# Griffin/Mamba trunk on one Trainium2 core: the first mixer's projection moved to the 512-column form

## What is computed

```python
def rglru_mixer(u, w_in, conv_w, conv_b, w_gate_r, b_gate_r, w_gate_i, b_gate_i, lam, w_out):
    xy = u @ w_in                                  # 2048 -> 4096: xr and yg
    xr, yg = jnp.split(xy, 2, axis=-1)
    yg = jax.nn.gelu(yg, approximate=True)
    xr = causal_dwconv(xr, conv_w, conv_b)         # 4 taps along the sequence
    xb = xr.reshape(bsz, S, LRU_HEADS, LRU_BLOCK)  # 8 heads of 256
    r = jax.nn.sigmoid(jnp.einsum('bshi,hij->bshj', xb, w_gate_r) + b_gate_r).reshape(bsz, S, LRU_WIDTH)
    i = jax.nn.sigmoid(jnp.einsum('bshi,hij->bshj', xb, w_gate_i) + b_gate_i).reshape(bsz, S, LRU_WIDTH)
    log_a = -LRU_C * r.astype(jnp.float32) * jax.nn.softplus(-lam.astype(jnp.float32))
    a = jnp.exp(log_a)
    mult = jnp.sqrt(-jnp.expm1(2.0 * log_a))
    bterm = mult * (i * xr).astype(jnp.float32)
    _, hs = lax.associative_scan(_lin_combine, (a, bterm), axis=1)
    return (hs.astype(u.dtype) * yg) @ w_out
```

## Time and profile before

| | us |
|---|---|
| median of 3 runs | 2684.93 |
| profiled execution, its own time | 2686.58 |
| its span, first to last instruction | 2684.9 |
| TensorE matmul busy | 2660.2 (99%) |
| VectorE busy | 1993.9 (74%) |
| ScalarE busy | 1394.8 (52%) |
| GpSimd busy | 282.4 (11%) |
| stage A1 | 8 to 227 us of the span |

### The profile page before, as it was taken

The page is one execution under the profiler, slowest core; times in us unless marked ns, Lnnn a source line. Parts: engine busy times, 40 slices in busy tenths (PEclk is TensorE's granted clock), DMA queues, the critical chain, the costliest instruction groups (busy, mean ns, idle before and its releaser), DMA issues.

```text
span 2684.9 us, 47929 instructions
## 1 busy us (share of the span) xinstructions
PE 2660.2 (99%) x16895; PEld 2399.2 (89%) x16895; DVE 1993.9 (74%) x2782; ACT 1394.8 (52%) x1924; POOL 282.4 (11%) x314
## 2 busy tenths in 40 slices
PE   8999999999999999999999999999999999999998
PEld 8999888888888888899998999988888888888887
DVE  7788776665666678888896788978666556667776
ACT  6776444444444445556764567644444444444454
POOL 1001300000000111100001000032000000001211
PEclk9999999999999999999999999999999999999999
DMA  6545555556655566555555555555555665555564
GB/s 217 180 169 191 180 196 189 190 173 188 204 190 190 194 189 198 188 175 189 182 187 187 197 181 184 188 186 189 191 189 173 188 204 191 189 189 175 188 202 138
DMA packets 157054, 502.54 MB, mean 187 GB/s; under 512 B 16848, under 2 KB 25360, under 8 KB 156816
## 3 DMA queue, kind: packets, MB, share of 16 engines
q1 hardware_dynamic: 156864, 501.04, 57.3%
q10 hardware_dynamic: 80, 0.07, 0.0%
HBM read 498.88 MB, written 2.16 MB: 187 GB/s over the span
## 4 chain that ended last, share of the span: by engine, by line
PE 89%; DVE 5%; ACT 3%; issue 1%; DMA 1%; SPq 0%; DVEq 0%; ACTq 0%
PE bank L408 51%; PE bank L410 26%; PE bank L390 4%; PE bank L392 4%; PE bank L391 4%; DVE wlo L904 2%; ACT whi L615 1%; DMA wraw<-in_A 1%; DVE arena L1114 1%; PE bank L576 0%; ACT L691 0%; DVE R L1005 0%; ACT arena L691 0%; ACT arena L700 0%; PE bank L580 0%
## 5 line engine op out<-in xcount | busy, mean ns | idle before, releaser
L408 PE MATMUL bank<-R,whi 128*128 128x512 f32 x5984 | 2084.9, 393 | 0.2 <-DVE wlo L904 0.2
L410 PE MATMUL bank<-R,wlo 128*128 128x256 f32 x5984 | 1674.1, 280 | 0.0
L904 DVE TENSOR_TENSOR wlo<-wraw,whi 128x1024 fp32r<-128x1024 f32 (+2 forms) x1008 | 1164.0, 1161 | 560.2 <-ACT whi L615 558.9
L615 ACT ACTIVATE whi<-wraw 128x1024 fp32r<-128x1024 f32 (+2 forms) x1008 | 984.1, 983 | 891.4 <-PE bank L410 794.1
L408 PEld LDWEIGHTS bank<-R,whi 128*128 128x128 f32 x5984 | 1120.4, 187 | 251.6 <-DVE wlo L904 0.6
L410 PEld LDWEIGHTS bank<-R,wlo 128*128 128x128 f32 x5984 | 1130.0, 189 | 0.1
L390 PE MATMUL bank<-R,whi 128*128 128x256 f32 x1376 | 392.9, 286 | 6.4 <-DVE wlo L904 5.3
L392 PE MATMUL bank<-R,wlo 128*128 128x256 f32 x1376 | 389.6, 283 | 0.0
L391 PE MATMUL bank<-R,whi 128*128 128x256 f32 x1376 | 389.3, 283 | 0.0
L390 PEld LDWEIGHTS bank<-R,whi 128*128 128x128 f32 x1376 | 262.4, 191 | 10.9 <-DVE wlo L904 6.7
L391 PEld LDWEIGHTS bank<-R,whi 128*128 128x128 f32 x1376 | 262.5, 191 | 0.2
(11 more groups left out here) (173 smaller groups left out, 1314.9 us busy)
## 6 DMA issues: line engine op xcount, KB each, us to landing
wraw<-in_F SPq DMA_DIRECT2D x352, 512.0 KB, 3.3
wraw<-in_B SPq DMA_DIRECT2D x224, 512.0 KB, 3.3
wraw<-in_A SPq DMA_DIRECT2D x96, 512.0 KB, 3.6
wraw<-in_F SPq DMA_DIRECT2D x128, 384.0 KB, 3.1
wraw<-in_F SPq DMA_DIRECT2D x128, 320.0 KB, 3.2
wraw<-in_PL SPq DMA_DIRECT2D x64, 512.0 KB, 3.7
arena<-cs_rows SPq DMA_DIRECT2D x8, 1024.0 KB, 6.4
arena<-in_gates SPq DMA_DIRECT2D x8, 512.0 KB, 3.7
```

The source lines that it names most:

```text
L408: nc.tensor.matmul(dst.rearrange("p (s t) -> p s t", s=2), whi[:, q % RING, cols], src[:, :, k, :], start=first, stop=False)
L410: mm = nc.tensor.matmul(dst[:, 0:SEQ], wlo[:, q % RING, cols], src[:, 0, k, :], start=False, stop=last)
L615: nc.scalar.activation(whi[:, slot, 0:w * BLOCK], wraw[:, slot, 0:w * BLOCK], ACT.Copy).then_inc(w_hi, 1)
L904: V.tensor_tensor(wlo[:, slot, 0:w * BLOCK], wraw[:, slot, 0:w * BLOCK], whi[:, slot, 0:w * BLOCK].bitcast(F32), ALU.subtract).then_inc(w_ ...
```

## The change

A1 joins WIDE, so its 512 blocks take one 512-column matmul and one of 256 instead of three of 256; banks 2, 3, 0, 1 are filled in both halves. At s = 1, 3, 5, 7 ScalarE now waits for the group's last piece (w_used) and copies the upper half of the bank into a_low (two buffers, a_half); VectorE waits for a_half, adds the lower half and a_low into xpad or yv, waits for its own result, and multiplies by rinv in place. In VectorE's program the yg groups now stand in front of the taps of the same q. tr and ti get two buffers, by hh, and decays waits for y_done of the head before, since av and sq still have one. lru_y moves from s = 7 to s = 1 of the next head, behind decays and gelu_square; y_low from s = 0 to s = 2. In A2 lru_y of the last heads stands at q = 1 and 5 and y_low at 2 and 6. The gate products keep their form. The core of the diff:

```diff
-LAST_HEAD = {0: (0, 1), 1: (2, 3), 2: (4,), 3: (5,), 4: (6,), 5: (7,)}
+LAST_HEAD = {0: (0, 1), 1: (2, 3), 2: (4,), 3: (5,), 4: (6,)}
-WIDE = ("A2", "F1", "F2", "B2")
+WIDE = ("A1", "A2", "F1", "F2", "B2")
...
+        tr = [tr, scratch(512).rearrange("p (j t) -> p j t", j=2)]
+        ti = [ti, scratch(512).rearrange("p (j t) -> p j t", j=2)]
+        a_low = scratch(512).rearrange("p (n t) -> p n t", n=2)
...
 # ScalarE
-                def decays(head):
+                def decays(head, hh):
                     act.wait_ge(gate_t, head * 4 + 2)
+                    if not isinstance(head, int) or head > 0:
+                        act.wait_ge(y_done, head)
...
-                    elif s == 7:
-                        lru_y(head, hh)
...
+                            if q in (1, 5):
+                                lru_y(LRU_HEADS - 2 + q // 5, q // 5)
...
                             head, hh, s = it * 2 + q // 8, q // 8, q % 8
+                            group = ({4: 0, 5: 1, 6: 2, 7: 3} if first and q < 8 else {1: 0, 3: 1, 5: 2, 7: 3}).get(s)
+                            if group is not None:
+                                act.wait_ge(w_used, HEAD_DONE[group] if first and q < 8 else p + 1)
+                                act.wait_ge(bank_free, it * 8 + ph["group0"] + hh * 4 + group + 3)
+                                nc.scalar.activation(a_low[:, group % 2, :], bank[BANKS4[group]][:, SEQ:2 * SEQ], ACT.Copy
+                                                     ).then_inc(a_half, 1)
...
+                            if s == 1 and not first:
+                                lru_y(head - 2, hh)
...
 # VectorE
-                            if q in (0, 6):
+                            if q in (2, 6):
                                 y_low(LRU_HEADS - 2 + q // 6, q // 6)
...
-                            if s == 0 and not first:
+                            if s == 2 and not first:
                                 y_low(head - 2, hh)
...
                             if group is not None:
-                                dve.wait_ge(w_used, HEAD_DONE[group] if first and q < 8 else p - s + 2 * group + 2)
-                                src = BANKS4[group]
-                            if group in (0, 1):
-                                j = group
-                                tile = head * 2 + j
-                                row = xpad[:, j, 3:3 + SEQ]
-                                V.tensor_tensor(row, bank[src][:, 0:SEQ], rinv[:], ALU.mult).then_inc(bank_free, 1)
+                                if group == 2 and not first:
+                                    dve.wait_ge(y_lo, head * 2 - 2)
+                                row = xpad[:, group, 3:3 + SEQ] if group < 2 else yv[:, hh, group - 2, :]
+                                dve.wait_ge(a_half, head * 4 + group + 1)
+                                own.link(V.tensor_tensor(row, bank[BANKS4[group]][:, 0:SEQ], a_low[:, group % 2, :], ALU.add))
+                                V.tensor_tensor(row, row, rinv[:], ALU.mult).then_inc(bank_free, 1)
...
-                            if group in (2, 3):
-                                if group == 2 and not first:
-                                    dve.wait_ge(y_lo, head * 2 - 2)
-                                row = yv[:, hh, group - 2, :]
-                                V.tensor_tensor(row, bank[src][:, 0:SEQ], rinv[:], ALU.mult).then_inc(bank_free, 1)
```

More of the change, by code:

```diff
@@ L239, in trunk @@
         z_t, exp_done, sc_done = sem("z_t"), sem("exp_done"), sem("sc_done")
-        turned = sem("turned")
+        turned, a_half = sem("turned"), sem("a_half")
         y_mm, y_read, ysq_done, gstat_mm, gvar_done, grinv_done = (sem("y_mm"), sem("y_read"), sem("ysq_done"),
@@ L684, in split_dt_weights, with gates @@
                                          ACT.Copy).then_inc(g_hi, 1)
-                def gates(head):
+                def gates(head, hh):
                     act.wait_ge(g_used, head + 1)
-                    for g, dst in ((0, tr), (1, ti)):
+                    for g, dst in ((0, tr[hh]), (1, ti[hh])):
                         for j in range(2):
@@ L693, in gates @@
                                                  scale=0.5).then_inc(gate_t, 1)
[L695 removed]
+                def decays(head, hh):
                     act.wait_ge(gate_t, head * 4 + 2)
+                    if not isinstance(head, int) or head > 0:
+                        act.wait_ge(y_done, head)
                     kk = [apar[:, at(head * 2 + j), 7:8].rearrange("p a b -> p (a b)") for j in range(2)]
                     for j in range(2):
[L700 removed]
+                        nc.scalar.activation(av[:, j, :], tr[hh][:, j, :], ACT.Exp, bias=kk[j], scale=kk[j]).then_inc(a_done, 1)
                     for j in range(2):
[L702 removed]
+                        nc.scalar.activation(tr[hh][:, j, :], tr[hh][:, j, :], ACT.Tanh, bias=kk[j], scale=kk[j]).then_inc(e_done, 1)
                     act.wait_ge(a_done, head * 2 + 2)
@@ L726, in chain_step @@
                     if s == 0:
-                        gates(head)
+                        gates(head, hh)
                     elif s == 1:
-                        decays(head)
+                        decays(head, hh)
                         gelu_square(head, hh)
@@ L1128, in chain_step @@
                         dve.wait_ge(e_done, head * 2 + 2)
-                        V.scalar_tensor_tensor(out=sq, in0=sq, scalar=1.0, in1=tr, op0=ALU.add, op1=ALU.mult
+                        V.scalar_tensor_tensor(out=sq, in0=sq, scalar=1.0, in1=tr[hh], op0=ALU.add, op1=ALU.mult
                                                ).then_inc(s_done, 1)
                         dve.wait_ge(gate_t, head * 4 + 4)
-                        V.scalar_tensor_tensor(out=ti, in0=ti, scalar=1.0, in1=xc[:, hh], op0=ALU.add, op1=ALU.mult
+                        V.scalar_tensor_tensor(out=ti[hh], in0=ti[hh], scalar=1.0, in1=xc[:, hh], op0=ALU.add, op1=ALU.mult
                                                ).then_inc(gated_done, 1)
@@ L1140, in chain_step @@
                         dve.wait_ge(mult_done, head + 1)
-                        V.tensor_tensor(ti, ti, sq, ALU.mult).then_inc(input_done, 1)
+                        V.tensor_tensor(ti[hh], ti[hh], sq, ALU.mult).then_inc(input_done, 1)
                         dve.wait_ge(input_done, head + 1)
                         for j in range(2):
-                            own.mark(V.tensor_tensor_scan(tr[:, j, :], av[:, j, :], ti[:, j, :], 0.0, ALU.mult, ALU.add))
+                            own.mark(V.tensor_tensor_scan(tr[hh][:, j, :], av[:, j, :], ti[hh][:, j, :], 0.0, ALU.mult, ALU.add))
                         own.need(own.latest())
-                        V.scalar_tensor_tensor(out=yv[:, hh], in0=tr, scalar=0.25, in1=ge, op0=ALU.mult, op1=ALU.mult
+                        V.scalar_tensor_tensor(out=yv[:, hh], in0=tr[hh], scalar=0.25, in1=ge, op0=ALU.mult, op1=ALU.mult
                                                ).then_inc(y_done, 1)
@@ L1369, in group_norm @@
                                                in1=grms[:], op0=ALU.mult, op1=ALU.mult).then_inc(yn_done, 1)
-                steps(dve, ph, body, own, {"A1": 14, "B1": 25, "F1": 6, "PL": 0, "F2": 4}.get(name, 8))
+                steps(dve, ph, body, own, {"A1": 22, "B1": 25, "F1": 6, "PL": 0, "F2": 4}.get(name, 8))
                 own.close()
```

## The result

The changed kernel takes 2694.36 us in the median of six runs (2692.91 to 2698.36), the kernel before 2684.61 beside it. The ratio is 1.0036, with a 95% interval of 1.0025 to 1.0046: slower by 0.36%. The forecast was 2687.2 us with a range from 2679 to 2692. The profiled execution has a span of 2692.8 us and took 2694.53, 7.95 us more than the profiled one of before. The medians are 9.75 apart: that profiled execution of before was itself 2.0 us above its median, and the one of after 0.2.

What follows compares the result with a forecast made beforehand. A cycle of VectorE and ScalarE was taken to bound A1. Last gates at 227.0 against 224.31, 2.7 us later, less A2's 0.4 gap, 2.3 net, counted from the 2684.93 median: 2687.2 us, range 2679 to 2692.

Steps and rivals of the forecast that it cites:

- a cycle of VectorE and ScalarE: In mid-stage A1 these two engines set the pace; the period goes from 26.19 to 27.13 us a head.
- the link through y: ScalarE's 3.15 us idle before copying y's high half in A1 goes; a longer link through TensorE replaces it.
- ScalarE's copy: Copying half a bank in each A1 group was taken at 0.36 us, between 0.3 and 0.6.
- VectorE's two operations: Each A1 group's added operation was priced at 0.58 us in the loop, 0.46 in the last, unrolled iteration.
- SyncE's and GpSimd's queues are not touched: Transfer queues in A1 and A2: claimed unchanged, graw still waiting for g_lo; moving later y halves costs TensorE nothing.
- the three periods of the loop: Three A1 heads at 27.13 us each, bringing the gates now at 172.38 to 174.0.
- the last two: Two A1 heads of the last iteration at 26.5 us each, ending at 227.0 against 224.31.
- the first iteration: Start of A1: a copy and two second operations cost 1.0 us, head 1's gates at 64.1; after 65.5 means wrong.
- The three late pieces: First iteration of A1: piece 8 waited 0.75 us for lo, and pieces 9 and 10 follow as tightly.
- its 0.4 us: TensorE's gap before 241.73 in A2, made by late decays, was to go.
- (b): Rival: TensorE sets the pace in A1, 25.4 us a head, 2676.4 us, or 2680 with half; chance 0.15.
- (c): Rival: ScalarE's path from the s = 1 copy to hi of s = 2 is longer, period 27.9, 2691.1 us; chance 0.22.

Runs made afterwards that it cites:

- late_copy_graw: Changed kernel with graw issued later and ScalarE's step 1 copy behind decays, the GELU square and lru_y: 2684.00 us, ratio 0.9995.
- after_graw_later: Changed kernel with graw issued three pieces later in SyncE's queue, at step 5 instead of 2: 2690.60 us, ratio 1.0021.
- form_only: Kernel before with the 512-column form, copies and additions in A1, but y's halves unmoved and one set of tr and ti: 2695.90 us, ratio 1.0039.
- late_copy: Changed kernel with ScalarE's step 1 copy behind decays, the GELU square and lru_y, graw not moved: 2693.13 us, ratio 1.0030.
- fold_graw: Changed kernel with graw issued later and the halves added by VectorE alone, without ScalarE's copies and waits: 2684.41 us, ratio 0.9997.
- mixed_one_head: Changed kernel with graw later, the step 1 copy behind decays, GELU square and lru_y, and head 0 in three-matmul form: 2681.53 us, ratio 0.9984.

## Why the prediction was wrong

**Right.** That a cycle of VectorE and ScalarE and not TensorE sets a head's time; that the link through y goes; that the new form is a small gain on TensorE. A block takes 0.353 us in the middle of A1 (late_copy_graw: 25.49 less 2.88 us of gates, over 64), so the form is worth 0.007 x 512 = 3.4 us where TensorE paces, where 5.1 had been taken. The estimate from the table of the Trainium skill ("TensorE: Matmul & The Clock Gate", section Back-to-back issue gap) was 1.3 us; the rows lie between the two. The new operations cost no more than was taken. ScalarE's copy is 375 ns in the mean, and the operation behind it starts 0.25 us after it (131.94 and 132.19), where 0.36 had been taken. VectorE's two operations are 416 and 425 ns, and the second starts 0.45 us after the first (150.39 and 150.84), where 0.58 had been taken in the loop (groups by line and form, 95 to 205 us, ScalarE's and then VectorE's):

```profile
L785 ACT ACTIVATE arena<-bank 128x256 f32<-128x256 f32 x16 | 6.0, 375 | 0.0
```

```profile
L1218 DVE TENSOR_TENSOR arena<-arena,rinv 128x256 f32<-128x256 f32 x16 | 6.8, 425 | 0.5
L1217 DVE TENSOR_TENSOR arena<-bank,arena 128x256 f32<-128x256 f32 x16 | 6.7, 416 | 0.0
```

From hi of step 2 (163.20) to the end of L1012 (177.33) the changed kernel takes 14.13 us, against 14.31 forecast.

**The step that failed** is the sentence "SyncE's and GpSimd's queues are not touched, and graw's transfer waits for g_lo as before". The queue wasn't touched, but what had covered it was: ScalarE's idle time of 3.15 us in front of L722, its wait for y. The prediction took that wait away and counted only the waits that ScalarE has for other engines, and not when the piece lands whose transfer stands behind graw. In the trace of before this could be read, as SyncE's own waits (for L1005, 6.4 us at the longest) and in the row at 151.40. The prediction put all of the 26.78 us of that head to the cycle of VectorE and ScalarE, and some 0.6 of it were the queue's. The queue link makes hi of step 2 start 13.3 us after L1012's end at the head of 150, and 14.2 at that of 121.69, where ScalarE waited 3.7 us for the piece; 12.82 was forecast. It costs the three periods of the loop 1.9 us beyond the forecast (83.3 instead of 81.4) and the last two 1.3 (54.3 instead of 53.0). after_graw_later, with the queue cleared, meets the forecast to 0.16 us a head.

**A term that was too small** is the first iteration. The gates of head 1 start at 65.78 instead of 64.1, behind the 65.5 that the prediction had named as the sign of it. The delay is 2.6 us, in place of 1.0, for which one copy and the second operations of two groups had been counted. The two traces show where it grows: VectorE's lo ahead of head 1's first group starts at 48.80 instead of 47.08, ScalarE's tap behind that group at 50.91 instead of 48.74, and its tap behind the next group at 57.43 instead of 54.80. So 1.7 us had come together by the end of head 0's work, and the second operations of head 1's first two groups added 0.45 each. The three late pieces at 36.82, 40.19 and 43.56 were named, and came as said:

```profile
36.82 0.50 PE L411 MATMUL bank<-R,whi 128*128 128x512 f32 x1 [1.18 <-DVE wlo L917]
...
40.19 0.49 PE L411 MATMUL bank<-R,whi 128*128 128x512 f32 x1 [0.29 <-DVE wlo L917]
...
43.56 0.50 PE L411 MATMUL bank<-R,whi 128*128 128x512 f32 x1 [0.32 <-DVE wlo L917]
```

The head that follows takes 28.35 us, the 28.5 of the forecast, and so 1.5 us of it are left at 94.13.

**The sum of the parts** at the last gate products: 1.5 us from the first iteration, 1.9 from the loop and 1.3 from the last iteration, 4.7 us together, are what lies between 227.0 forecast and 231.74. A2 gave back its 0.4 us as forecast. From the first norm's matmul after A2 to the end the changed kernel takes 0.9 us more than before (2362.0 against 2361.1). Nothing of the change lies there, and the profiles of all kernels lie between 2360.8 and 2362.2, so this is read as scatter. The forecast counted from the median of 2684.93. The profiled execution of before was 1.65 us above that and the one of after 0.17 above its own median, which gives the last 1.5 us of the 7.2 by which 2694.36 lies over 2687.2.

**The rivals.** (b) was wrong for the change as it is, and names the period once both links are out. (c) said slower by another mechanism, ScalarE's path dearer than taken; its prices didn't come. The link that came had no rival of its own, and the range had no room for it.

**A stretch at the lower clock.** In the changed kernel the gate products of head 1 take 4.43 us instead of 2.9, most of the 24 matmuls starting 0.21 us after each other instead of 0.12:

```profile
66.54 0.41 PE L395 MATMUL bank<-R 128*128 128x256 f32 x1
66.75 0.41 PE L393 MATMUL bank<-R 128*128 128x256 f32 x1
```

The busy time by engine of that window, with the granted clock behind GpSimd's (x0), gives the cause:

```profile
66.50:69.50 3.00, 3.00 (x16) 3.00 (x15) 1.74 (x4) 2.97 (x4) 0.00 (x0) 0.50 0.93 343
```

The granted clock was 0.50 there, the lower of TensorE's two levels (1.2 instead of 2.4 GHz), and 1.00 before and after. TensorE had stood 2.17 us in front of these products. The same happened in form_only (twice), late_copy (at the gates of 121.66), late_copy_graw and fold_graw, each time with 0.50 granted behind an idle time of 1.85 to 2.82 us. It did not happen in after_graw_later behind 2.12 us, nor in mixed_one_head behind 1.72 us, nor in the five kernels with head 1 in the old form, where no idle time in front of gate products is over 1.33 us. On the path it cost little where it fell on head 1: the next gates follow after 28.35 us, against 28.00 in after_graw_later at the full clock. What decides between the idle times that bring it and those that don't, no run tells.

## What to carry to other kernels

When an edit takes a wait away from an engine, look for everything that landed during that wait, transfers included, and go through the queue that issues them: a transfer behind a waiting one in the same queue inherits its wait. Where two links lie beside each other, taking one away gives only the distance to the other: in the changed kernel 3.8 us and 1.2 us by one alone, 10.4 by both (medians, of different sets); in the kernel before nothing that can be measured by either the moves or graw's later issue, 3 us by both. And an instruction that waits for TensorE belongs in ScalarE's program behind the work that doesn't need it.

## What the runs showed of the hardware

Not expected: TensorE's granted clock fell to 0.50 for a few microseconds in five of the twelve profiles, behind 1.85 to 2.82 us in which TensorE stood idle, while the mean over each profiled execution stays at 0.997 to 0.998. There 256-column matmuls start every 0.21 us instead of 0.12.

From the issue of a weight piece behind graw to the split that waited for it took 4.3 and 5.3 us in the changed kernel (150.29 to 154.63 and 121.89 to 127.17), and 5.5 in the one head of before (145.88 to 151.40).

As expected from the rows of before otherwise: an operation of VectorE or ScalarE on 256 elements from half a bank costs 0.38 to 0.42 us, and overlaps its neighbours by 0.1.
